# A trunk of RWKV-7 and dilated attention: gate weights loaded into a freed mix, one panel beside the weight ring, the bias copies in six parts

## The chip, the cores and the metric

The kernel runs on one core of one Trainium2 chip. The core has five engines that run side by side, each through its own list of instructions: TensorE (PE in the profile; matmuls, with PEld for the loads of its stationary operand), VectorE (DVE), ScalarE (ACT), GpSimd (POOL) and SyncE (SP), which here only issues DMAs. They wait for each other by semaphores. The metric is the device time of one launch in microseconds; a kernel's time is the median of several runs.

## What is computed

One RWKV-7 time-mixing layer, a feed-forward layer, one dilated-attention layer and a second feed-forward layer, on 512 tokens of width 1024. The change lies in the first of them and in the data that the attention's bias needs:

```python
xx = jnp.pad(h, ((0, 0), (1, 0), (0, 0)))[:, :-1] - h
x_mix = h[None] + xx[None] * mu[:, None, None, :]
r, k, v = (x_mix[c] @ w_rkv[c] for c in range(3))
xw, xa, xg = x_mix[3], x_mix[4], x_mix[5]
w = -jax.nn.softplus(-(w0 + jnp.tanh(xw @ w1) @ w2)) - 0.5
decay = jnp.exp(-jnp.exp(w))
a = jax.nn.sigmoid(a0 + (xa @ a1) @ a2)
g = jax.nn.sigmoid(xg @ g1) @ g2
...
y = rwkv7_scan(r, decay, k, v, -kk, kk * a)     # state, token by token
out = ((group_norm(y) + bonus) * g) @ w_o
...
logits = logits + bias[None, None, None]        # attention: a bias by head and distance
```

Here `w1`, `a1`, `g1` are the first, narrow halves of the decay, removal and output gates (64, 64 and 160 columns), `w2`, `a2`, `g2` the second ones.

## The kernel before

**First projections.** The activations lie transposed, in eight chunks of 128 rows by 512 tokens. The weights come as *panels* of 128 x 1024 numbers (512 KB, `stream[p]`), each the weights of one output tile: panels 0 to 2 for the first keys and values, 3 to 10 for the receptance, 11 (`PAN_WA`) for the decay and removal gates together, 12 and 13 (`PAN_G`) for the output gate. From 14 on (`PAN_PROJ`) come the keys and values of the later head pairs. SP loads panel p into slot p mod 2 of a ring, `O_RAW`, as soon as the panel that had the slot, p - 2, is through. For most panels that means "split": ScalarE rounds the panel to a high half (`split_high`) and VectorE subtracts that to get the low half (`split_low`), both into rings of three, and TensorE takes 24 matmuls for a tile (`product`). A few panels, 11 and those from 14 on among them, are read by TensorE straight from the ring, and there the slot is free when the tile is done (semaphore `dense`). Tiles go alternately into two PSUM banks, which ScalarE empties (`take`); the next tile but one waits for that (`freed`).

Panel 11's tile is `decay_and_gate` on TensorE; ScalarE empties it in two pieces, Tanh for the decay half and a plain copy for the other. Tiles 12 and 13 are emptied with Sigmoid. ScalarE holds one set of function tables at a time, and a change of set is an instruction of its own (ACT_TABLE_LOAD).

**The loop.** Then a loop over k from -1 to 8 works on the eight head pairs, with parts of three pairs interleaved: `gates`, `key_norm_ready`, `first_inverse`, the scores and so on of pair k+1, the inverse of pair k, the walk over the chunks of pair k-1. I call the loop body with k = 0 round 0. Into it are spread `project(k, 0)` to `project(k, 15)`, eight matmul steps each of two further panels, which keep TensorE busy between the small matmuls. The order on each engine is written out by hand; nothing is scheduled afterwards.

The gates' second weights (`lora_out`) come in pieces of 128 KB per head pair, two slots for the decay and removal gates (`O_LWA`, `gate_weights`) and two for the output gate (`O_LWG`, `output_gate_weights`). SP issues them, and the constants of the loop (`O_CM`, "the mask", with the reset pattern that VectorE's scan and GpSimd's start wait for), after the last projection tile.

**The bias.** The attention layer far behind needs every bias row of 384 numbers 128 times, shifted; for that 48 rows in DRAM (`bias_rows`) are copied 128 times each into `bias_copies`, by three DMAs from DRAM to DRAM of 3072 KB. They too stand in SP's list, behind the first gate weights; SP waits for them when the attention layer starts.

Of the kernel before, what the change touches and what calls it, by code (L numbers as in the profile page):

```python
# [160 lines left out]
O_LWA = O_CM + N_CM  # L161
O_LWG = O_LWA + 2 * 2 * P
O_AR = O_LWG + 2 * 2 * P
# [7 lines left out]
O_EP = O_CC + S  # L171
# [54 lines left out]
def trunk(nc, xT, stream, lora_out, pvec, const, rel33, out):  # L226
    with ExitStack() as ctx:
# [178 lines left out]

        def full(eng, t):

            eng.wait_ge(s["dense"], TILE_AT[t])
# [7 lines left out]
        def _(sp):  # L417
# [7 lines left out]
            def panel(p):  # L425
                if p >= RAW and is_split(p - RAW):
                    sp.wait_ge(s["w_lo"], split_of(p - RAW) + 1)
                elif p >= RAW:
                    sp.wait_ge(s["dense"], PANEL_AT[p - RAW])
                sp.dma_start(f(O_RAW + p % RAW * 1024, 1024), stream[p]).then_inc(s[f"w_raw{p % RAW}"], 16)  # L430

            for p in range(PAN_PROJ + RAW):
                panel(p)
                if p == 1:
                    sp.dma_start(f(O_OH, 3 * 384, 0, 33), const[0:33, C_OH:C_OH + 3 * 384]).then_inc(s["oh_in"], 16)
                    sp.dma_start(f(O_REL, 48, 0, 33), rel33).then_inc(s["oh_in"], 16)
                    sp.dma_start(con(C_ID), const[:, C_ID:C_ID + P]).then_inc(s["con_in"], 16)
                    sp.dma_start(con(C_HEAD, 2 * P), const[:, C_HEAD:C_HEAD + 2 * P]).then_inc(s["con_in"], 16)
            full(sp, T_WO0 - 1)
            sp.dma_start(f(O_CM, N_CM), const[:, C_SCORE:C_OH]).then_inc(s["mask_in"], 16)  # L440

# [12 lines left out]
            gate_weights(0)  # L454
            gate_weights(1)
            output_gate_weights(0)
            output_gate_weights(1)
            sp.wait_ge(s["bias_dma"], 48)
            for g in range(3):
                rows = bias_rows[g * 16 * 384:(g + 1) * 16 * 384]  # L460
                copies = bias_copies[g * 16 * P * 384:(g + 1) * 16 * P * 384]
                sp.dma_start(copies.rearrange("(h i u) -> h i u", h=16, i=P),
                             bass.AP(tensor=rows.tensor, offset=g * 16 * 384, ap=[[384, 16], [0, P], [1, 384]]))\
                    .then_inc(s["bias_rep"], 16)
            for k in range(-1, NHP - 1):
# [1662 lines left out]
```

## Time and profile before

| | |
|---|---|
| median of 3 runs | 1932.83 us (1930.52 to 1936.12) |
| the profiled execution | 1931.57 us, of it 1929.8 us span |
| granted TensorE clock, mean | 0.972 of 2.4 GHz |
| TensorE busy | 1821.2 us (94%), 15682 matmul records |
| VectorE, ScalarE, GpSimd busy | 932.1, 781.3, 203.8 us |
| DMA | 155.04 MB, mean 80 GB/s |
| `bias_copies` from `bias_rows` | 3 DMAs of 3072.0 KB |

A matmul in fp32 shows as two records, each of about the length of one pass. In the timelines equal instructions that follow each other are merged, with their number behind an x; what stands in brackets is the idle time of the engine just before, and what ended it. A line L503 or L506 is a helper through which every matmul goes, so groups of matmuls are known by their time, number and shape. For SP the length of a row runs from the first of its issues to the end of the last, waits between them included. The granted clock is 1.00 at 2.4 GHz and 0.50 at 1.2 GHz.

### The profile page before, as it was taken

The numbers are of one execution on the slowest core, as the hardware profiler recorded it, in microseconds if no ns is written. First come the engines' busy times: TensorE is split into PE (matmuls) and PEld (weight loads), VectorE is DVE, ScalarE is ACT, GpSimd is POOL, SyncE is SP. The second block draws the span as 40 slices with busy tenths as digits, with TensorE's granted clock in tenths as the row PEclk, the third lists the DMA queues.
The fourth block names the chain that finished last, engine by engine and source line by source line (L and its number), as shares of the span: only waits on it lengthen the run. The fifth ranks groups of instructions, "written<-read, shape, count | busy, mean of one in ns | idle before, by whom it ended". The sixth has DMA issues, their size and how long they took to land.

```text
span 1929.8 us, 36430 instructions
## 1 busy us (share of the span) xinstructions
PE 1821.2 (94%) x15682; PEld 1407.4 (73%) x15682; DVE 932.1 (48%) x1585; ACT 781.3 (40%) x1326; POOL 203.8 (11%) x180
## 2 busy tenths in 40 slices
PE   8978999987799999999999999999999799999999
PEld 3745555655578888888887777777787688888887
DVE  6624555555444444434445554654654554444422
ACT  4333444434233222322446556556656543222211
POOL 0022333334110000000010111111111000000000
PEclk9989999987789999999999999999999899999999
DMA  3281111000222233323232222222222133323322
GB/s 121 77 260 43 34 30 30 28 16 3 70 72 94 97 98 98 99 99 98 88 99 77 77 68 76 77 77 66 79 75 77 33 99 98 99 88 102 100 95 97
DMA packets 57544, 155.04 MB, mean 80 GB/s; under 512 B 5591, under 2 KB 22535, under 8 KB 57384
## 3 DMA queue, kind: packets, MB, share of 16 engines
q1 hardware_dynamic: 57288, 152.63, 24.6%
q8 instruction: 125, 2.05, 0.4%
q14 instruction: 35, 0.29, 0.0%
q10 hardware_dynamic: 96, 0.07, 0.0%
HBM read 150.51 MB, written 11.61 MB: 84 GB/s over the span
## 4 chain that ended last, share of the span: by engine, by line
PE 67%; ACT 4%; issue 1%; DVE 0%; POOL 0%; ACTq 0%; DVEq 0%
PE bank L503 66%; PE bank L506 2%; ACT f L1433 2%; ACT f L1446 1%; ACT f L1420 0%; ACT r L1411 0%; ACT f L1407 0%; ACT f L1438 0%; POOL f L2045 0%; POOL f L2049 0%; DVE f L1899 0%; POOL f L2047 0%; DVE f L1910 0%; DVE r L1916 0%; DVE f L1697 0%
## 5 line engine op out<-in xcount | busy, mean ns | idle before, releaser
L503 PE MATMUL bank<-r 128*128 128x512 f32 x5616 | 1304.2, 392 | 7.0 <-DVE r L1916 3.7
L503 PEld LDWEIGHTS bank<-r 128*128 128x128 f32 x5616 | 1050.9, 188 | 241.3 <-issue 18.1
L503 PE MATMUL bank<-f 64*64 64x64 f32 (+6 forms) x9634 | 475.5, 259 | 78.2 <-DVE f L1637 16.6
L503 PEld LDWEIGHTS bank<-f 64*64 64x64 f32 (+3 forms) x9634 | 308.1, 146 | 235.3 <-issue 110.7
L1506 DVE TENSOR_TENSOR r<-f,r 128x1024 fp32r<-128x1024 f32 x230 | 282.9, 1231 | 390.4 <-ACT r L1122 390.4
L1122 ACT ACTIVATE r<-f 128x1024 fp32r<-128x1024 f32 x230 | 240.7, 1047 | 151.6 <-PE bank L503 138.2
L2074 POOL TENSOR_TENSOR r<-f,r 128x512 fp32r<-128x512 f32 x48 | 62.2, 1295 | 885.8 <-ACT r L1411 885.8
L1390 ACT ACTIVATE r<-f 128x512 fp32r<-128x512 f32 x44 | 27.8, 632 | 218.1 <-DVE f L1809 218.1
L1840 DVE TENSOR_TENSOR f<-bank,f 128x512 f32<-128x512 f32 x72 | 56.0, 777 | 87.6 <-PE bank L503 84.7
L1637 DVE TENSOR_TENSOR f<-bank,f 64x512 f32<-64x512 f32 x80 | 55.1, 689 | 66.6 <-PE bank L503 65.4
L506 PE MATMUL bank<-f 128*128 128x128 f32 x432 | 65.4, 281 | 20.2 <-ACT f L1446 14.3
L506 PEld LDWEIGHTS bank<-f 128*128 128x128 f32 x432 | 49.0, 141 | 42.2 <-ACT f L1446 26.7
L1420 ACT ACTIVATE f<-bank,f 128x512 f32<-128x512 f32 x48 | 32.9, 686 | 100.0 <-PE bank L503 100.0
L1387 ACT ACTIVATE f<-f 128x512 f32<-128x512 f32 x44 | 27.8, 632 | 112.4 <-DVE f L1799 112.4
L1446 ACT ACTIVATE f<-bank 128x512 f32<-128x512 f32 (+1 forms) x64 | 36.4, 568 | 89.6 <-PE bank L506 89.6
L1803 DVE TENSOR_TENSOR f<-bank,f 128x512 f32<-128x512 f32 x44 | 30.4, 691 | 78.8 <-PE bank L503 78.8
L1433 ACT ACTIVATE f<-f 128x256 f32<-128x256 f32 (+1 forms) x128 | 61.4, 481 | 2.3 <-DVE f L1882 2.3
L1856 DVE SCALAR_TENSOR_TENSOR f<-f 128x512 f32<-128x512 f32 x32 | 37.3, 1166 | 39.5 <-ACT f L1422 39.5
L1873 DVE CUSTOM_DVE_ANT_0 f<-bank,f 128x256 f32<-128x256 f32 (+1 forms) x128 | 44.4, 404 | 11.8 <-PE bank L503 11.7
L1194 ACT ACTIVATE f<-bank 128x512 f32<-128x512 f32 (+1 forms) x48 | 27.7, 594 | 53.6 <-PE bank L503 38.3
L1376 ACT ACTIVATE r<-f 128x512 fp32r<-128x512 f32 x24 | 15.2, 633 | 83.0 <-DVE f L1782 83.0
L1645 DVE COPY f<-bank 128x512 f32<-128x512 f32 (+1 forms) x40 | 27.5, 689 | 42.7 <-PE bank L503 42.7
(108 smaller groups left out, 959.5 us busy)
## 6 DMA issues: line engine op xcount, KB each, us to landing
f<-stream SPq DMA_DIRECT2D x247, 512.0 KB, 3.4
bias_copies<-bias_rows SPq DMA_DIRECT2D x3, 3072.0 KB, 24.7
f<-xT SPq DMA_DIRECT2D x16, 256.0 KB, 4.3
f<-lora_out SPq DMA_DIRECT2D x16, 128.0 KB, 3.7
f<-bias_copies SPq DMA_DIRECT2D x16, 128.0 KB, 3.2
f<-bias_copies SPq DMA_DIRECT2D x32, 64.0 KB, 2.9
outT<-f SPq DMA_DIRECT2D x8, 256.0 KB, 4.5
f<-const SPq DMA_DIRECT2D x1, 576.0 KB, 3.7
```

Of the source, the lines that this page charges most:

```text
L503: return nc.tensor.matmul(out, lhsT, rhs, start=start, stop=stop, skip_group_check=True)
L506: return nc.tensor.transpose(out, in_, con(C_ID))
L1122: A(r(O_WHI + q % PAN * 1024, 1024), f(O_RAW + p % RAW * 1024, 1024), ACT.Copy)\
L1420: free(A(f(O_QS), banks[4][:, :], ACT.Ln, bias=kol(K_EPS), scale=1.0 / HD), 4)
L1433: A(tile, tile, ACT.Exp, bias=f(sm + 8 + n, 1), accum_out=f(sm + 16 + n, 1))\
L1446: free(A(f(O_PT + n % N_PT * S, w), banks[5][:, 0:w], ACT.Copy), 5)
L1506: TT(r(O_WLO + q % PAN * 1024, 1024), f(O_RAW + panel_of(q) % RAW * 1024, 1024), rf(O_WHI + q % PAN * 1024, 1024), ALU.subtract).then_inc( ...
L1637: TT(bc(half(O_XI, e), (CH, 8), (1, CH)), banks[2 + e][CH * e:CH * (e + 1), :].rearrange("p (t j) -> p t j", t=8), bc(lev, (0, 8), (1, CH) ...
L1840: TT(out, in0, in1, ALU.mult).then_inc(freed(t), 1)
L1856: STT(by_residue(to), bc(f(O_QR + n % 2 * S), (4, P), (1, 4)), gain, bc(f(O_QS), (4, P), (1, 4)), ALU.mult, ALU.mult).then_inc(s["qk_norm" ...
L1873: ins = V.tensor_tensor_reduce(out=f(O_P + h * 4 * S + n * 2 * P + first, w), in0=banks[b][:, e * 2 * P + first:(e + 1) * 2 * P], in1=f(O_ ...
L2074: TT(r(O_QL), f(O_QQ), rf(O_QH), ALU.subtract).then_inc(s["q_sq_lo"], 1)
```

## The change

Panel 11 is loaded into `O_TG`, the place in which the output gate's Sigmoid results are put later, with a semaphore of its own (`w_wa`). It no longer takes a slot of the ring, so panel 13 waits for panel 9, the last one that had its slot; the ring's counts are one lower from there on for that slot (`raw_in`). The slots for `lora_out` move into the place of the receptance mix (`O_XM`), which is free when tile 10 is done, and their first four loads are issued there, before panel 14. ScalarE loads the sigmoid tables before it waits for tile 11, copies first, then takes Tanh, and splits panel 13 behind that. The three copies become six of half the size, issued one in each of rounds 0 to 5 behind the round's panels.

```diff
@@ places in SBUF
-O_LWA = O_CM + N_CM
-O_LWG = O_LWA + 2 * 2 * P
-O_AR = O_LWG + 2 * 2 * P
+O_AR = O_CM + N_CM
...
-O_EP = O_CC + S
+O_LWA = O_CC + S
+O_LWG = O_LWA + 2 * 2 * P
+O_EP = O_LWG + 2 * 2 * P
+assert O_XM <= O_LWA and O_EP <= O_XM + KC * S
@@ all engines
+        def raw_in(eng, p):
+            early = p > PAN_WA and (p - PAN_WA) % RAW == 0
+            eng.wait_ge(s[f"w_raw{p % RAW}"], 16 * (p // RAW + 1 - early))
@@ SP
             def panel(p):
-                if p >= RAW and is_split(p - RAW):
-                    sp.wait_ge(s["w_lo"], split_of(p - RAW) + 1)
-                elif p >= RAW:
-                    sp.wait_ge(s["dense"], PANEL_AT[p - RAW])
+                held = p - RAW - (RAW if p - RAW == PAN_WA else 0)
+                if p == PAN_WA:
+                    sp.dma_start(f(O_TG, 1024), stream[p]).then_inc(s["w_wa"], 16)
+                    return
+                if held >= 0 and is_split(held):
+                    sp.wait_ge(s["w_lo"], split_of(held) + 1)
+                elif held >= 0:
+                    sp.wait_ge(s["dense"], PANEL_AT[held])
...
             for p in range(PAN_PROJ + RAW):
+                if p == PAN_PROJ:
+                    full(sp, PAN_WA - 1)
+                    for hp in range(2):
+                        gate_weights(hp)
+                        output_gate_weights(hp)
                 panel(p)
...
-            gate_weights(0)
-            gate_weights(1)
-            output_gate_weights(0)
-            output_gate_weights(1)
-            sp.wait_ge(s["bias_dma"], 48)
-            for g in range(3):
-                rows = bias_rows[g * 16 * 384:(g + 1) * 16 * 384]
-                copies = bias_copies[g * 16 * P * 384:(g + 1) * 16 * P * 384]
-                sp.dma_start(copies.rearrange("(h i u) -> h i u", h=16, i=P),
-                             bass.AP(tensor=rows.tensor, offset=g * 16 * 384, ap=[[384, 16], [0, P], [1, 384]]))\
+            def copy_bias(n):
+                lo = n * 8 * 384
+                copies = bias_copies[lo * P:(lo + 8 * 384) * P]
+                sp.dma_start(copies.rearrange("(h i u) -> h i u", h=8, i=P),
+                             bass.AP(tensor=bias_rows.tensor, offset=lo, ap=[[384, 8], [0, P], [1, 384]]))\
                     .then_inc(s["bias_rep"], 16)
             for k in range(-1, NHP - 1):
                 if k + 3 < NHP:
                     gate_weights(k + 3)
                 for p in (PAN_PROJ + 2 * (k + 2), PAN_PROJ + 2 * (k + 2) + 1):
                     if p < PAN_WO0 + RAW:
                         panel(p)
+                if 0 <= k < 6:
+                    if k == 0:
+                        sp.wait_ge(s["bias_dma"], 48)
+                    copy_bias(k)
                 if k >= 1:
                     output_gate_weights(k + 1)
@@ TensorE, decay_and_gate
-                pe.wait_ge(s[f"w_raw{t % RAW}"], 16 * (t // RAW + 1))
+                pe.wait_ge(s["w_wa"], 16)
...
-                    w = O_RAW + t % RAW * 1024 + c * P
+                    w = O_TG + c * P
@@ ScalarE
-                split_high(min(t + LEAD, PAN_PROJ - 1))
+                if t != PAN_WA:
+                    split_high(min(t + LEAD, PAN_PROJ - 1))
                 for i in MIXED_AT.get(t, []):
                     round_mixed(i)
                 if t == PAN_WA:
+                    nc.scalar.preload_act_table_set("sigmoid_and_others")
                     full(act, t)
-                    A(f(O_TW, S, 0, LORA), banks[t % 2][0:LORA, :], ACT.Tanh)
-                    A(f(O_TA, S, LORA, P), banks[t % 2][LORA:P, :], ACT.Copy).then_inc(freed(t), 1)
+                    A(f(O_TA, S, LORA, P), banks[t % 2][LORA:P, :], ACT.Copy)
+                    A(f(O_TW, S, 0, LORA), banks[t % 2][0:LORA, :], ACT.Tanh).then_inc(freed(t), 1)
+                    split_high(PAN_PROJ - 1)
```

The rest of the diff puts `raw_in` in the places where TensorE and ScalarE waited for a ring slot, and doubles the count that SP waits for before the attention's bias (`bias_rep`, 96 for 48).

SP's list before, from panels 5 to 12 in the first row, panel 13 in the second, to the loads of the first pass of the loop (a stream row is a panel; the 128x1152 row is the mask; of `lora_out`, L445 is `gate_weights` and L451 `output_gate_weights`):

```order
L430 DMA f<-stream 128x1024 [waits w_lo] x8
L430 DMA f<-stream 128x1024 [waits dense]
L430 DMA f<-stream 128x1024 [waits w_lo] x2
L440 DMA f<-const 128x1152 [waits dense]
L445 DMA f<-lora_out 128x2x128 x2
L451 DMA f<-lora_out 128x2x128 x2
L462 DMA bias_copies<-bias_rows 2048x1x384 [waits bias_dma]
L462 DMA bias_copies<-bias_rows 2048x1x384 x2
L445 DMA f<-lora_out 128x2x128 [waits a_ps]
L430 DMA f<-stream 128x1024 [waits dense] x2
```

The same stretch of SP's list now; L434 is panel 11, and the row behind it is panels 12 and 13:

```order
L440 DMA f<-stream 128x1024 [waits w_lo] x6
L434 DMA f<-stream 128x1024
L440 DMA f<-stream 128x1024 [waits w_lo] x2
L445 DMA f<-lora_out 128x2x128 [waits dense]
L451 DMA f<-lora_out 128x2x128
L445 DMA f<-lora_out 128x2x128
L451 DMA f<-lora_out 128x2x128
L440 DMA f<-stream 128x1024 [waits w_lo] x2
L467 DMA f<-const 128x1152 [waits dense]
L445 DMA f<-lora_out 128x2x128 [waits a_ps]
L440 DMA f<-stream 128x1024 [waits dense] x2
```

The four gate weights stand before panels 14 and 15 and the mask, where they stood behind them, and panel 13 waits for a low half (`w_lo`) where it waited for tile 11 (`dense`). The copies are gone from here.

SP's list now, from the loads of round 0 through those of round 2:

```order
L445 DMA f<-lora_out 128x2x128 [waits a_ps]
L440 DMA f<-stream 128x1024 [waits dense] x2
L474 DMA bias_copies<-bias_rows 1024x1x384 [waits bias_dma]
L445 DMA f<-lora_out 128x2x128 [waits a_ps]
L440 DMA f<-stream 128x1024 [waits dense] x2
L474 DMA bias_copies<-bias_rows 1024x1x384
L451 DMA f<-lora_out 128x2x128 [waits g_ps]
```

Each copy stands behind the two panels of its round, and before the output gate's weights where there are any.

ScalarE's list before, from tile 9 to the first gates (L1158 is `take`, L1122 the split of panels 12 and 13, L1140 the rounding of the output gate's mix, L1186 and L1187 Tanh and the copy, L1194 the gates' Sigmoid):

```order
L1158 ACTIVATE f<-bank 128x512 [waits dense]
L1122 ACTIVATE r<-f 128x1024 [waits dense,w_raw0]
L1140 ACTIVATE r<-f 128x512 [waits mix_t] x2
L1158 ACTIVATE f<-bank 128x512 [waits dense]
L1122 ACTIVATE r<-f 128x1024 [waits dense,w_raw1]
L1186 ACT_TABLE_LOAD
L1186 ACTIVATE f<-bank 64x512 [waits dense]
L1187 ACTIVATE f<-bank 64x512
L1158 ACT_TABLE_LOAD
L1158 ACTIVATE f<-bank 128x512 [waits dense] x2
L1204 ACTIVATE f<-f 128x512 [waits tile_free1,tile_free0]
L1194 ACTIVATE f<-bank,f 128x512 [waits w_ps]
```

The same stretch now (L1175, L1139, L1157, L1205 the copy, L1206 Tanh, L1214):

```order
L1175 ACTIVATE f<-bank 128x512 [waits dense]
L1139 ACTIVATE r<-f 128x1024 [waits dense,w_raw0]
L1157 ACTIVATE r<-f 128x512 [waits mix_t] x2
L1175 ACTIVATE f<-bank 128x512 [waits dense]
L1203 ACT_TABLE_LOAD
L1205 ACTIVATE f<-bank 64x512 [waits dense]
L1206 ACTIVATE f<-bank 64x512
L1139 ACTIVATE r<-f 128x1024 [waits dense,w_raw1]
L1175 ACTIVATE f<-bank 128x512 [waits dense] x2
L1224 ACTIVATE f<-f 128x512 [waits tile_free1,tile_free0]
L1214 ACTIVATE f<-bank,f 128x512 [waits w_ps]
```

The split of panel 13 has moved behind Tanh and the copy, these two have changed places, the first table load stands ahead of the wait for `dense`, and the second is gone.

## Rows read from the trace of the kernel before

**Rows 1.** Part 4 of the page, the chain by engine.

```profile
PE 67%; ACT 4%; issue 1%; DVE 0%; POOL 0%; ACTq 0%; DVEq 0%
```

**Rows 2.** Timeline of TensorE, 95 to 300: start, us, instructions, [idle before <- releaser].

```profile
95.98 5.85 PE L503 MATMUL bank<-r 128*128 128x512 f32 x24
103.41 5.85 PE L503 MATMUL bank<-r 128*128 128x512 f32 x24 [1.57 <-ACT f L1187]
113.56 2.08 PE L503 MATMUL bank<-f 64*128 64x512 f32 x4 [4.31 <-DMA f<-lora_out]
116.38 11.37 PE L503 MATMUL bank<-f 128*128 128x512 f32 x20 [0.74 <-ACT f L1194]
128.53 7.97 PE L503 MATMUL bank<-f 128*128 128x512 f32 x140 [0.78 <-ACT f L1316]
...
143.12 1.16 PE L503 MATMUL bank<-f 64*64 64x64 f32 x64 [2.13 <-ACT f L1194]
149.29 7.71 PE L503 MATMUL bank<-f 128*128 128x512 f32 x110 [5.00 <-DMA f<-stream]
...
193.57 7.92 PE L503 MATMUL bank<-f 64*64 64x64 f32 x198 [2.13 <-ACT f L1194]
...
240.27 9.52 PE L503 MATMUL bank<-f 64*64 64x64 f32 x198 [2.13 <-ACT f L1194]
```

**Rows 3.** Windows: length, busy time of engines, granted clock, DMA share, GB/s.

```profile
116.38:121.58 5.20, 5.20 (x6) 2.16 (x7) 2.77 (x3) 3.26 (x5) 3.09 (x3) 0.51 1.04 325
121.58:143.12 21.54, 18.22 (x195) 8.42 (x193) 5.64 (x9) 4.49 (x9) 10.08 (x9) 1.00 0.98 316
149.29:153.00 3.71, 3.71 (x32) 2.56 (x36) 0.00 (x0) 0.25 (x1) 0.00 (x0) 0.61 0.02 8
143.12:187.37 44.25, 37.39 (x953) 24.91 (x953) 20.81 (x32) 15.85 (x30) 12.28 (x11) 0.92 0.14 45
193.57:231.94 38.37, 36.99 (x1037) 25.23 (x1037) 23.43 (x41) 17.58 (x33) 15.11 (x14) 1.00 0.07 19
```

**Rows 4.** Timeline of ScalarE, 95 to 130.

```profile
99.79 1.06 ACT L1122 ACTIVATE r<-f 128x1024 fp32r<-128x1024 f32 x1 [10.12 <-DMA f<-stream]
100.87 1.28 ACT L1186 ACT_TABLE_LOAD   x1
102.16 0.59 ACT L1186 ACTIVATE f<-bank 64x512 f32<-64x512 f32 x1
...
109.30 0.60 ACT L1158 ACTIVATE f<-bank 128x512 f32<-128x512 f32 x1 [4.03 <-PE bank L503]
```

**Rows 5.** Timeline of SP's DMA issues, 40 to 700.

```profile
109.29 0.33 SPq L440 DMA_DIRECT2D f<-const  x1
...
111.68 14.52 SPq L462 DMA_DIRECT2D bias_copies<-bias_rows  x3
126.24 11.28 SPq L445 DMA_DIRECT2D f<-lora_out  x1
137.56 2.75 SPq L430 DMA_DIRECT2D f<-stream  x2
...
170.06 20.68 SPq L430 DMA_DIRECT2D f<-stream  x2
...
214.93 22.50 SPq L430 DMA_DIRECT2D f<-stream  x2
```

**Rows 6.** Timeline of VectorE, 105 to 200.

```profile
113.10 0.17 DVE L1701 TENSOR_SCALAR f<-f 128x8 f32<-128x8 f32 x1 [10.99 <-DMA f<-const]
...
119.10 1.22 DVE L1590 TENSOR_TENSOR_SCAN f<-f 128x512 f32<-128x512 f32 x1
```

**Rows 7.** Timeline of GpSimd, 105 to 200.

```profile
117.11 0.77 POOL L1983 TENSOR_SCALAR f<-f 128x512 f32<-128x512 f32 x1 [116.67 <-ACT f L1194]
...
120.39 1.06 POOL L1993 TENSOR_TENSOR f<-f 128x512 f32<-128x512 f32 x1 [1.17 <-DVE f L1590]
...
126.21 1.27 POOL L2013 TENSOR_TENSOR f<-f 128x512 f32<-128x512 f32 x1
```

More of the change, by code:

```diff
@@ L425, in panel @@
             def panel(p):
-                if p >= RAW and is_split(p - RAW):
-                    sp.wait_ge(s["w_lo"], split_of(p - RAW) + 1)
-                elif p >= RAW:
-                    sp.wait_ge(s["dense"], PANEL_AT[p - RAW])
-                sp.dma_start(f(O_RAW + p % RAW * 1024, 1024), stream[p]).then_inc(s[f"w_raw{p % RAW}"], 16)
[L432 to L440, printed above, removed]
+                held = p - RAW - (RAW if p - RAW == PAN_WA else 0)
[6 more added lines that the diff above has]
+                    sp.wait_ge(s["dense"], PANEL_AT[held])
+                sp.dma_start(f(O_RAW + p % RAW * 1024, 1024), stream[p]).then_inc(s[f"w_raw{p % RAW}"], 16)
             def gate_weights(hp):
@@ L452, in output_gate_weights @@
                              lora_out[:, 2:4, hp * P:(hp + 1) * P]).then_inc(s[f"lwg_in{hp % 2}"], 16)
-            gate_weights(0)
-            gate_weights(1)
-            output_gate_weights(0)
-            output_gate_weights(1)
-            sp.wait_ge(s["bias_dma"], 48)
-            for g in range(3):
-                rows = bias_rows[g * 16 * 384:(g + 1) * 16 * 384]
-                copies = bias_copies[g * 16 * P * 384:(g + 1) * 16 * P * 384]
-                sp.dma_start(copies.rearrange("(h i u) -> h i u", h=16, i=P),
-                             bass.AP(tensor=rows.tensor, offset=g * 16 * 384, ap=[[384, 16], [0, P], [1, 384]]))\
+            for p in range(PAN_PROJ + RAW):
+                if p == PAN_PROJ:
[3 more added lines that the diff above has]
+                        output_gate_weights(hp)
+                panel(p)
+                if p == 1:
+                    sp.dma_start(f(O_OH, 3 * 384, 0, 33), const[0:33, C_OH:C_OH + 3 * 384]).then_inc(s["oh_in"], 16)
+                    sp.dma_start(f(O_REL, 48, 0, 33), rel33).then_inc(s["oh_in"], 16)
+                    sp.dma_start(con(C_ID), const[:, C_ID:C_ID + P]).then_inc(s["con_in"], 16)
+                    sp.dma_start(con(C_HEAD, 2 * P), const[:, C_HEAD:C_HEAD + 2 * P]).then_inc(s["con_in"], 16)
+            full(sp, T_WO0 - 1)
+            sp.dma_start(f(O_CM, N_CM), const[:, C_SCORE:C_OH]).then_inc(s["mask_in"], 16)
+            def copy_bias(n):
[3 more added lines that the diff above has]
+                             bass.AP(tensor=bias_rows.tensor, offset=lo, ap=[[384, 8], [0, P], [1, 384]]))\
                     .then_inc(s["bias_rep"], 16)
@@ L482, in _ @@
                     if hp == 0 and h == 0:
-                        sp.wait_ge(s["bias_rep"], 48)
+                        sp.wait_ge(s["bias_rep"], 96)
                         sp.wait_ge(s["hd_lo"], FC)
@@ L547, in plain @@
                     pe.wait_ge(freed(t), t // 2)
-                pe.wait_ge(s[f"w_raw{t % RAW}"], 16 * (t // RAW + 1))
+                raw_in(pe, t)
                 for c in range(KC):
@@ L556, in decay_and_gate @@
                 pe.wait_ge(freed(t), t // 2)
-                pe.wait_ge(s[f"w_raw{t % RAW}"], 16 * (t // RAW + 1))
+                pe.wait_ge(s["w_wa"], 16)
                 for c in range(KC):
@@ L587, in project @@
                 if c == 0:
-                    pe.wait_ge(s[f"w_raw{p % RAW}"], 16 * (p // RAW + 1))
+                    raw_in(pe, p)
                     if n:
@@ L1118, in split_high @@
                     p = panel_of(q)
-                    act.wait_ge(s[f"w_raw{p % RAW}"], 16 * (p // RAW + 1))
+                    raw_in(act, p)
                     if q >= PAN:
```

## The prediction

> **What bounds the kernel now.** I read the page first: the chain that ended last runs for 67% of the span through TensorE's matmuls, and no other engine has more than 4% of it [rows 1]. So only a stretch in which TensorE waits, or in which its clock is low, can give time back. The change touches the end of the first projections and the first round of the RWKV loop, so the second view is TensorE's timeline there [rows 2]. The reader is to see three waits. Tile 13, the last projection tile (24 matmuls), starts 1.57 us after tile 12 ended and waits for ScalarE's line 1187. The first four matmuls of the loop, from the decay and gate weights, start 4.31 us after tile 13 and wait for a load of lora_out. And in round 0 TensorE is done with 64 small matmuls at 144.28 and then waits 5.00 us for a panel of stream.
>
> The third view is a set of windows [rows 3]: the granted clock is at 0.51, the 1.2 GHz level, from 116.38 to 121.58 behind the first two waits, at 1.00 from there to 143.12, and at 0.61 on average from 149.29 to 153.00 behind the third wait. Round 0 from its 64 matmuls to its scores takes 44.25 us; round 1, with more matmuls in it, 38.37.
>
> The fourth view is who holds TensorE up. On ScalarE [rows 4] the split of panel 13 stood in front of Tanh. It began at 99.79 after 10.12 us of waiting for the panel, whose load could only start when the decay tile, tile 11, was through with the slot; a table load of 1.28 us followed, and only then Tanh and the copy that free the bank. On SP [rows 5] the mask is asked for when tile 13 ends (109.29) and the gate weights behind it. Then three copies occupy SP for 14.52 us and the next gate weights for 11.28 more, so the panel that round 0 needs at 144.28 is asked for at 137.56 and is there at 149.29. Each of these causes is something that the change moves.
>
> **Tile 13 without its wait.** Panel 11 goes outside the ring, so panel 13 waits only for panel 9 and is in place long before. The sigmoid table is loaded ahead of the wait for tile 11, where ScalarE waits anyway; copy, Tanh and split follow. From tile 11's end, about 96.0 (the next row starts at 95.98), I count two evacuations of 0.59 (the row at 102.16), the split of 1.06, and for VectorE's half as much as for ScalarE's: 3.3 us, so the weights are ready at 99.3 and tile 12 ends at 95.98 + 5.85 = 101.83. Tile 13 starts there: 1.57 us saved, with 2.5 us of cover left. The second table load, between Tanh and Sigmoid, is gone; it lay beside tile 13 and counts nothing.
>
> **The loop's start without the load.** The four loads of lora_out are asked for when tile 10 ends; two whole tiles and tile 13 lie between that and their use. What remains late is ScalarE's evacuation of tile 13: 0.04 + 0.60 [rows 4], and about 0.13 for the signal. Tile 13 ends at 101.83 + 5.85 = 107.68, so the four matmuls start at 108.45 instead of 113.56, 5.11 us earlier with the 1.57 in it. The loads now stand on SP ahead of panels 14 and 15, which start later by four issues; the mask's issue took 0.33, and these panels are needed after 111. No cost.
>
> **The clock.** With 0 and 0.77 us of waiting in place of 1.57 and 4.31, I take it that TensorE keeps 2.4 GHz. The rows bound it: the four matmuls cost 2.08 at the low level and half, 1.04, at the high one; the 5.20 us at 0.51 become 2.60. Behind the four, TensorE still waits 0.74 for ScalarE. So the block of 20 passes starts at 108.45 + 1.04 + 0.74 = 110.23, takes 11.37 - 2.60 = 8.77 and ends at 119.00; with the 0.78 behind it the next block starts at 119.78 and not at 128.53.
>
> **What is late next there.** The mask is still asked for at the end of tile 13, 109.26 before. VectorE had it 3.84 us later [rows 6], so now at 107.68 + 3.84 = 111.52, and GpSimd can start 0.17 + 0.23 later, at 111.92, though ScalarE would let it start at 111. Its chain to the scaled vectors that the first inverse needs (the product that ends at 126.21 + 1.27 = 127.48) took 10.37 us from 117.11 [rows 7], of which 1.17 were a wait for VectorE's scan. The scan ended at 120.32, 3.94 after the block of 20 began; now at 114.2 at the latest, when GpSimd asks for it at about 114.0. That leaves 9.2 us: 121.15. TensorE would get there at 119.78 plus two passes (0.88), 120.66, and waits half a microsecond. Before, it got there at 129.41 and found the product ready. **Gain up to here: 129.41 - 121.15 = 8.26 us.**
>
> **Round 0 without the panel's wait.** The panel is asked for when its slot is free, at 119.0, with no copy in front. Even if it took the 11.7 us of before it would be there at 130.7, and it is needed at about 136.0 (144.28 less 8.26). The 5.00 us go, and with them the low clock behind: (1 - 0.61) x 3.71 = 1.45. **6.45 us.** Rounds 0 and 1 compared give 44.25 - 38.37 = 5.88 with more work in round 1, which fits.
>
> **The copies, one a round.** The trace has no copy of the new size. Three old ones took SP 14.52, 4.84 each; a new one takes between half of that and all of it, and I take half. SP has room: the second panel of a pair is out by 190.74 and the next panel is asked for at 214.93 [rows 5]. The bytes, 1.57 MB at the 325 GB/s of the first window in [rows 3], take 4.8 us. The panel in front of a copy is needed when the next round is half through its projection, which is also when the next panel is asked for, 24 us later. So I cost the copies at nothing; a gain is excluded, as rounds from 1 on have no such wait to lose, and the far end is rival C.
>
> **The sum.** 8.26 + 6.45 = 14.71. The profiled execution took 1931.57 us (span 1929.8), 1.26 below the median of 1932.83 and within the runs shown: 1931.57 - 14.71 = 1916.86, so 1917. What lies behind round 0 is a chain that starts from it and moves along.
>
> **Rivals.**
> B, the clock stays low. Four waits of 0.5 to 0.8 us remain between 107 and 121, and one of 2.13 in every round [rows 2]. Behind such a wait the same 198 matmuls take 7.92 us in round 1 and 9.52 in round 2, 1.60 more. If the first stretch stays at 1.2 GHz, its gain is 5.11 and not 8.26, and if round 0 falls as round 2 did, 1.60 more goes: 5.11 + 6.45 - 1.60 = 9.96, 1921.6. For it: TensorE is at the low level here now. Against it: the wait of 0.78 at 128.53 left the clock at 1.00. The Trainium skill (TensorE: Matmul & The Clock Gate, "A second HAM failure mode: psum-queue depth-cycling") says that TensorE can swing between its two clocks when it idles briefly between groups of matmuls; by that rule B's 1921.6 stands in place of 1917. The trace agrees for the 2.13 us waits in some rounds and not for the shorter ones, which is why B has the smaller chance.
>
> C, the copies get in the way of panels: slower. They share the queue. If each of the six did to a round what the three did to round 0, that would cost 6 x 6.45 = 38.7: 1916.9 + 38.7 = 1955.6. It decides from the point where a panel beside a copy lands more than 24 us after its request; in round 0 one took 11.7 behind what was left of three copies of twice the size, which speaks against it. The Trainium skill (DMA: Bandwidth & Descriptors, "Queues, rings and completion order") says that a DMA engine takes what one issuer queued in ring order; the trace agrees in so far as that panel came late behind the copies. By that rule C's 1955.6 stands wherever the cover is shorter than I read.
>
> D, another wait takes a removed one's place: the panel's turns into one for ScalarE's copy of the projected key, or GpSimd's chain is longer than 9.2. Half the gain is left, 6.5 to 8.3 us: 1923 to 1925. Against it: in round 1 the same 64 matmuls are followed by others without a wait.
>
> E, later low-clock stretches swallow it, as they need not fall on the same rounds when all is earlier: 1.6 us each, three or four of them against the change. With D's half gain that is no change, about 1930.
>
> **Chances.** The forecast 0.67, its own range 1911 to 1922 (three such stretches either way, and the scatter of the runs); B 0.16; D 0.09; E 0.04; C 0.04. About 0.3%, 5.8 us, is what this measurement can tell from no change. Faster: 0.67 + 0.16 + 0.07 of D = 0.90; same 0.06; slower 0.04. The range is 1910 to 1924, with B inside.
>
> **What would show it.** Right: tile 13 follows tile 12 without a wait; under 1 us in front of the loop's first four matmuls; the full clock from 108 to 121; the block that began at 128.53 begins near 119.8; no wait for stream in round 0, and some 38 us for it; one table load, ahead of Tanh. Wrong: a clock near 0.5 from 110 to 118 (B), a wait for stream in rounds 1 to 6 (C), one of several us for ScalarE or GpSimd in round 0 (D), or later rounds that grew (E).

## The result and the profile after

The changed kernel takes 1918.91 us (median of 4 runs, 1914.41 to 1919.21), the kernel before 1933.38 (4 runs, 1930.52 to 1936.12). The ratio is 0.992, 95% interval 0.9899 to 0.9941: 14.5 us are gone. The profiled execution took 1919.21 us, of it 1917.4 span; against the profiled one of before, 1931.57, that is 12.4 less. A second set of runs is among the experiments (a1): 0.9922 (0.9909 to 0.9935).

The chain of the page says what it said before [rows 1], with one point more for TensorE:

```profile
PE 68%; ACT 4%; issue 1%; DVE 0%; POOL 0%; ACTq 0%; DVEq 0%
```

TensorE's timeline from tile 12 on answers to [rows 2]:

```profile
96.65 11.42 PE L520 MATMUL bank<-r 128*128 128x512 f32 x48
108.80 1.13 PE L520 MATMUL bank<-f 64*128 64x512 f32 x4 [0.73 <-issue]
110.67 6.28 PE L520 MATMUL bank<-f 128*128 128x512 f32 x14 [0.74 <-ACT f L1214]
117.43 2.81 PE L520 MATMUL bank<-f 128*128 128x512 f32 x6 [0.48 <-DVE f L1626]
...
122.78 6.94 PE L520 MATMUL bank<-f 64*64 64x64 f32 x138 [0.66 <-POOL f L2033]
130.14 4.08 PE L520 MATMUL bank<-f 64*64 64x128 f32 x40 [0.42 <-issue]
136.34 8.97 PE L520 MATMUL bank<-f 64*64 64x64 f32 x174 [2.13 <-ACT f L1214]
...
181.96 7.92 PE L520 MATMUL bank<-f 64*64 64x64 f32 x198 [2.13 <-ACT f L1214]
...
275.94 9.50 PE L520 MATMUL bank<-f 64*64 64x64 f32 x198 [2.13 <-ACT f L1214]
```

Tiles 12 and 13 are one row now, 48 matmuls without a wait. The loop's first four matmuls follow 0.73 us behind, and no row waits for a load of lora_out or for a panel of stream. The first inverse, which began at 129.41 (two matmuls into the row of 128.53), begins at 122.78, and the scores (the row of 40) at 130.14, where before they began at 136.91. All of this stands 0.67 us late from tile 12 on (96.65 for 95.98), which I don't count to the change: tile 11, in front of it, began anywhere from 88.30 to 90.28 in profiled executions below whose instructions up to there are the same as here (89.63). I take the 0.67 out where I compare places; the whole time has it in it.

The windows (columns as in [rows 3]):

```profile
97.00:122.78 25.78, 22.39 (x75) 12.94 (x73) 7.29 (x7) 10.28 (x17) 9.22 (x8) 1.00 0.21 67
136.34:175.75 39.41, 37.64 (x953) 25.32 (x953) 20.81 (x32) 15.86 (x30) 12.29 (x11) 0.96 0.06 17
181.40:190.30 8.90, 8.35 (x204) 6.26 (x205) 5.80 (x10) 5.28 (x8) 3.09 (x3) 1.00 0.56 200
```

The granted clock is 1.00 in the whole first stretch, where it was 0.51 for 5.20 us. Round 0 takes 39.41 us and not 44.25, but at a clock of 0.96. The last row is the stretch of the first copy, whose packets run from 181.39 to 190.29; I come back to it.

ScalarE beside tiles 11 to 13, for [rows 4]:

```profile
90.35 1.28 ACT L1203 ACT_TABLE_LOAD   x1
96.77 0.59 ACT L1205 ACTIVATE f<-bank 64x512 f32<-64x512 f32 x1 [5.13 <-PE bank L520]
97.37 0.59 ACT L1206 ACTIVATE f<-bank 64x512 f32<-64x512 f32 x1
97.86 1.05 ACT L1139 ACTIVATE r<-f 128x1024 fp32r<-128x1024 f32 x1
```

The table load stands inside ScalarE's wait for tile 11, and copy, Tanh and split follow each other from 96.77. VectorE's half of that split is this row:

```profile
98.94 1.22 DVE L1526 TENSOR_TENSOR r<-f,r 128x1024 fp32r<-128x1024 f32 x1 [9.12 <-ACT r L1139]
```

SP's issues, for [rows 5]:

```profile
91.18 0.47 SPq L451 DMA_DIRECT2D f<-lora_out  x1
91.69 8.84 SPq L440 DMA_DIRECT2D f<-stream  x2
108.10 0.33 SPq L467 DMA_DIRECT2D f<-const  x1
...
120.27 13.24 SPq L440 DMA_DIRECT2D f<-stream  x2
...
179.17 0.75 SPq L474 DMA_DIRECT2D bias_copies<-bias_rows  x1
```

The panels of round 0 are asked for from 120.27 to 133.51, with nothing in front, and the copies go out behind the panels of later rounds, at 179.17 first, where one takes SP 0.75 us. VectorE in the first stretch, for [rows 6]:

```profile
111.91 0.17 DVE L1721 TENSOR_SCALAR f<-f 128x8 f32<-128x8 f32 x1 [11.74 <-DMA f<-const]
...
112.59 1.63 DVE L1610 TENSOR_TENSOR_SCAN f<-f 128x512 f32<-128x512 f32 x1
114.14 1.68 DVE L1621 SCALAR_TENSOR_TENSOR f<-f 128x512 f32<-128x512 f32 x1
115.74 1.54 DVE L1626 SCALAR_TENSOR_TENSOR f<-f 128x512 f32<-128x512 f32 x1
```

GpSimd in the same stretch, for [rows 7]:

```profile
112.38 0.77 POOL L2003 TENSOR_SCALAR f<-f 128x512 f32<-128x512 f32 x1 [111.94 <-DVE f L1721]
113.23 2.04 POOL L2007 TENSOR_TENSOR f<-f 128x512 f32<-128x512 f32 x1
115.24 1.50 POOL L2013 TENSOR_TENSOR f<-f 128x512 f32<-128x512 f32 x1
...
121.37 1.26 POOL L2033 TENSOR_TENSOR f<-f 128x512 f32<-128x512 f32 x1
```

Here is the part that did not go by plan. The scan took 1.22 us before [rows 6] and takes 1.63. GpSimd's product beside it (L2007) takes 2.04, and its next one (L2013) 1.50, which took 1.06 [rows 7]. VectorE's unit key (L1621) takes 1.68. In the kernel before, that first product and the unit key were these:

```profile
117.96 1.26 POOL L1987 TENSOR_TENSOR f<-f 128x512 f32<-128x512 f32 x1
120.64 1.36 DVE L1601 SCALAR_TENSOR_TENSOR f<-f 128x512 f32<-128x512 f32 x1 [0.32 <-ACT f L1218]
```

### The profile page after: what moved, and what is told of

Read it like the earlier page. It is cut to its first block, busy times and chain, and to the rows that moved or that the text cites. A ratio compares the mean times of both kernels' runs of the same rounds, so it can differ in the third digit from the quotient of the medians.

```text
span 1917.4 us, 36432 instructions
## 1 busy us (share of the span) xinstructions
PE 1816.0 (95%) x15682; PEld 1404.8 (73%) x15682; DVE 933.5 (49%) x1585; ACT 779.8 (41%) x1325; POOL 204.9 (11%) x180
## 4 chain that ended last, share of the span: by engine, by line
PE 68%; ACT 4%; issue 1%; DVE 0%; POOL 0%; ACTq 0%; DVEq 0%
PE bank L520 66%; PE bank L523 2%; ACT f L1453 2%; ACT f L1466 1%; ACT f L1440 0%; ACT r L1431 0%; ACT f L1427 0%; ACT f L1458 0%; POOL f L2065 0%; POOL f L2069 0%; DVE f L1919 0%; POOL f L2067 0%; DVE r L1936 0%; DVE f L1930 0%; DVE f L1717 0%
## 5 line engine op out<-in xcount | busy, mean ns | idle before, releaser
L520 PE MATMUL bank<-f 64*64 64x64 f32 (+6 forms) x9634 | 470.6, 258 | 72.6 <-DVE f L1657 16.9
L1139 ACT ACTIVATE r<-f 128x1024 fp32r<-128x1024 f32 x230 | 240.7, 1047 | 143.0 <-PE bank L520 138.1
L1860 DVE TENSOR_TENSOR f<-bank,f 128x512 f32<-128x512 f32 x72 | 56.0, 778 | 87.6 <-PE bank L520 84.7
L1823 DVE TENSOR_TENSOR f<-bank,f 128x512 f32<-128x512 f32 x44 | 30.4, 692 | 78.8 <-PE bank L520 78.8
L1819 DVE TENSOR_TENSOR f<-bank,f 128x512 f32<-128x512 f32 x44 | 30.4, 692 | 35.0 <-PE bank L520 29.1
L1214 ACT ACTIVATE f<-bank 128x512 f32<-128x512 f32 (+1 forms) x48 | 27.7, 594 | 47.0 <-PE bank L520 32.1
```

The source lines that it names most:

```text
L520: return nc.tensor.matmul(out, lhsT, rhs, start=start, stop=stop, skip_group_check=True)
L1139: A(r(O_WHI + q % PAN * 1024, 1024), f(O_RAW + p % RAW * 1024, 1024), ACT.Copy)\
L1860: TT(out, in0, in1, ALU.mult).then_inc(freed(t), 1)
```

## The experiments

Each kernel was timed in rounds with the kernel before on the same chip; ratios are to that, with the 95% interval. The times named in the expectations are for a chip on which the kernel before takes 1933 us, so gains are compared, not times. The kernels of a group shared a chip: e1 to e4 (before: 1930.03 us); a1, e5, e6 and e8 (1932.21); e7, e9 and e10 (1928.64). The [rows] named here are those ahead of the prediction.

**e1, the copies in front again.** The changed kernel, with the three old copies at their old place.

```diff
+            sp.wait_ge(s["bias_dma"], 48)
+            for g in range(3):
+                rows = bias_rows[g * 16 * 384:(g + 1) * 16 * 384]
...
-                if 0 <= k < 6:
-                    if k == 0:
-                        sp.wait_ge(s["bias_dma"], 48)
-                    copy_bias(k)
```

> The kernel after, but with the three old copies at their old place, behind the mask and ahead of the loop's loads. Theory (the parts depend on each other): the copies start some 3 us earlier than before, so the panel of round 0 lands near 146 while TensorE wants it near 137; the 8 us won ahead of it turn into a longer wait for stream, about 8.6 us. Gain against before only 3 to 4 us, about 1930. Rival (the parts simply add): 8.3 us won stay, 6.45 of round 0 are not: about 1925.

Measured: 1926.3 us, 0.9985 (0.9971 to 0.9999). TensorE in its round 0:

```profile
135.44 1.16 PE L515 MATMUL bank<-f 64*64 64x64 f32 x64 [2.13 <-ACT f L1209]
144.31 7.95 PE L515 MATMUL bank<-f 128*128 128x512 f32 x110 [7.72 <-DMA f<-stream]
```

SP's issues before that, in the same kernel:

```profile
107.45 13.24 SPq L474 DMA_DIRECT2D bias_copies<-bias_rows  x3
120.74 11.46 SPq L445 DMA_DIRECT2D f<-lora_out  x1
```

By the times 3 to 4 us are gained, as the theory has it and not the rival's 8.3. The whole first stretch is early, as in the changed kernel: the scores of the first pass start at 129.23, 7.68 before those of the kernel before. Part of that is lost in round 0: the panel lands at 144.3, TensorE is there at 136.6 and waits 7.72, and the scores of round 0 are 4.68 early (182.69 for 187.37). The panel of before landed at 149.29 [rows 2]. So the early start alone is worth little, because the panel's time is set by the copies.

**e2, the copies alone.** The kernel before, with the copies one a round.

```diff
-            for g in range(3):
-                rows = bias_rows[g * 16 * 384:(g + 1) * 16 * 384]
...
+            def copy_bias(n):
+                lo = n * 8 * 384
...
+                if 0 <= k < 6:
+                    if k == 0:
+                        sp.wait_ge(s["bias_dma"], 48)
+                    copy_bias(k)
```

> The kernel before with nothing but the copies moved: six of half the size, one a round. Theory: the 5.00 us wait for stream in round 0 and 1.45 us of low clock behind it go, nothing else: 6.45 us, about 1927. The first two waits (1.57 and 4.31) and the low clock behind them stay. Rival (the copies moved into the rounds cost something there, a wait for stream or lora_out in rounds 1 to 6): less than 5 us gained, 1929 or more. Together with the run without moved copies, the theory says that the two gains add up to some 10 us, not to the 14.5 of both.

Measured: 1923.62 us, 0.9968 (0.9955 to 0.998), 6.2 to 6.4 us less. TensorE's timeline:

```profile
103.36 5.85 PE L508 MATMUL bank<-r 128*128 128x512 f32 x24 [1.53 <-ACT f L1192]
113.50 1.81 PE L508 MATMUL bank<-f 64*128 64x512 f32 x4 [4.29 <-DMA f<-lora_out]
...
142.52 7.43 PE L508 MATMUL bank<-f 64*64 64x64 f32 x174 [2.13 <-ACT f L1199]
```

The two waits of the first stretch stand, the one for stream is gone, and round 0 from 142.52 to its scores at 180.71 takes 38.19 us. The term of 6.45 is confirmed by itself. With e1, the two parts alone give 3 and 6 us, 9 or 10 together, and both at once 14.5 to 15: much of the first part's gain is paid out only when the second has removed the wait behind it.

**e3, the gate weights late.** The changed kernel, with the four lora_out loads behind the mask again.

```diff
-                if p == PAN_PROJ:
-                    full(sp, PAN_WA - 1)
-                    for hp in range(2):
-                        gate_weights(hp)
-                        output_gate_weights(hp)
...
+            gate_weights(0)
+            gate_weights(1)
+            output_gate_weights(0)
+            output_gate_weights(1)
```

> The kernel after, but the four first loads of lora_out at their old place, behind the mask. Theory: TensorE waits some 4.3 us for lora_out before the loop, and its clock falls behind that: the four matmuls take 2 us and the block behind them stays half-way at the low level, so the loss is 3.5 for the wait and up to 3 for the clock, 6 us, about 1925. Rival: the first inverse is bound by the mask and GpSimd's chain, not by TensorE, so most of it is hidden: TensorE's clock falls but the loss is 2 to 4 us, about 1922.

Measured: 1921.51 us, 0.9959 (0.9946 to 0.9971). TensorE:

```profile
112.09 2.08 PE L519 MATMUL bank<-f 64*128 64x512 f32 x4 [4.34 <-DMA f<-lora_out]
114.92 10.79 PE L519 MATMUL bank<-f 128*128 128x512 f32 x20 [0.74 <-ACT f L1213]
```

The wait for lora_out is back, and with it the low clock: the granted clock is 0.50 from 112.09 to 116.00, the four matmuls take 2.08 for 1.13, the block behind them 10.79. The scores come at 134.86, 4.7 us later than in the changed kernel, 5.0 with tile 11 set to the same place. By the ratios (0.9959 for 0.9922 in a1) it is 7 us, which is the theory's 6 rather than the rival's 2 to 4; the 2 us by which this is more than in the trace are not accounted for. This is the largest piece of the first stretch, and its loss of clock goes with it.

**e4, panel 11 in the ring.** The changed kernel, with panel 11 in the ring and ScalarE's old order at tile 11.

```diff
-            early = p > PAN_WA and (p - PAN_WA) % RAW == 0
+            early = 0
...
-                    nc.scalar.preload_act_table_set("sigmoid_and_others")
...
-                    A(f(O_TA, S, LORA, P), banks[t % 2][LORA:P, :], ACT.Copy)
-                    A(f(O_TW, S, 0, LORA), banks[t % 2][0:LORA, :], ACT.Tanh).then_inc(freed(t), 1)
-                    split_high(PAN_PROJ - 1)
+                    A(f(O_TW, S, 0, LORA), banks[t % 2][0:LORA, :], ACT.Tanh)
+                    A(f(O_TA, S, LORA, P), banks[t % 2][LORA:P, :], ACT.Copy).then_inc(freed(t), 1)
```

> The kernel after, but panel 11 in the ring and ScalarE's old order around Tanh with its two table loads. Theory: the wait of 1.57 us in front of tile 13 is back, and nothing else changes: about 1920.5, clock at 1.00 until 121. Rival: with 1.57, 0.75 and 0.75 us of waiting close together the clock falls to 0.5 there and the loss is 3 to 5 us: 1922 to 1924.

Measured: 1918.23 us, 0.9943 (0.9928 to 0.9959). TensorE:

```profile
104.01 5.86 PE L516 MATMUL bank<-r 128*128 128x512 f32 x24 [1.54 <-ACT f L1200]
```

Tile 13 waits 1.54 us, the scores come at 131.90, 1.76 later, and the clock stays at 1.00 from 104 to 124.55. By the trace the step is worth what it was given, 1.6; by the time (0.9943 against 0.9922 for a1 below, with intervals that overlap) that can't be told from nothing. The ring and ScalarE's order are undone together here, so which of the two brings the wait back is not shown.

**a1, the changed kernel again**, for the kernels of the second group.

> The kernel after, unchanged, as the measure for the runs beside it and for the four that went before, on a chip whose kernel before takes about 1930. Theory: ratio 0.992 to 0.993 as at first, about 1916; the panel in the ring cost 1.6 us of that, the late gate loads 5 to 6, the copies in front 10. In its trace VectorE's scan takes near 1.6 us and GpSimd's product beside it near 2.0, as at first (1.22 and 1.26 in the kernel before).

Measured: 1915.86 us (1915.44 to 1918.59), 0.9922 (0.9909 to 0.9935).

**e5, the reset pattern early.** The pattern that the scan and GpSimd's start wait for is cut off the mask and loaded with the gate weights, so that GpSimd starts when ScalarE lets it.

```diff
+                    sp.dma_start(f(O_RESET), const[:, C_RESET:C_OH]).then_inc(s["reset_in"], 16)
...
-            dve.wait_ge(s["mask_in"], 16)
+            dve.wait_ge(s["reset_in"], 16)
...
-            pool.wait_ge(s["mask_in"], 16)
```

> The kernel after, with the mask cut in two: the reset pattern that the scan reads (512 columns) goes into a further part of the freed receptance mix and is loaded with the gate weights; the other 640 columns come when the mask came, and VectorE and GpSimd wait for them only at the first inverse. Theory (the mask holds up GpSimd's start): GpSimd starts some 1 us earlier, at 111.4 on the first trace's times instead of 112.38, and TensorE's first inverse is 1.0 to 1.3 us earlier: about 1 us faster than the kernel after. Rival (VectorE and GpSimd slow each other when they run at the same time, and that sets the chain): the start is earlier but the scan and the product beside it take as long or longer, and less than 0.5 us comes of it.

Measured: 1916.62 us, 0.992 (0.9903 to 0.9938), no difference to a1. VectorE's scan in it:

```profile
111.77 2.17 DVE L1613 TENSOR_TENSOR_SCAN f<-f 128x512 f32<-128x512 f32 x1
```

GpSimd's first three operations in it:

```profile
110.74 0.77 POOL L2007 TENSOR_SCALAR f<-f 128x512 f32<-128x512 f32 x1 [110.30 <-ACT f L1217]
111.59 1.27 POOL L2011 TENSOR_TENSOR f<-f 128x512 f32<-128x512 f32 x1
114.02 1.48 POOL L2017 TENSOR_TENSOR f<-f 128x512 f32<-128x512 f32 x1 [1.16 <-DVE f L1613]
```

GpSimd starts 0.96 us earlier (tile 11 set to the same place), and its product takes 1.27, but the scan beside it takes 2.17, GpSimd's next product waits 1.16 for that, and the first inverse gains only 0.55. The mask is not the whole of the lateness.

**e8, GpSimd's product behind the scan.** One wait more in the first pass, so that the product and the scan don't overlap.

```diff
+                if hp == 0:
+                    pool.wait_ge(s["cs"], 1)
```

> The kernel after, but for the first head pair GpSimd waits for VectorE's scan before its second operation, the product that ran beside the scan. Theory (two engines slow each other): the scan goes back to 1.2 us from 1.6 and GpSimd's product to about 1.3 from 2.0, so that the chain ends no later, within 0.7 us. Rival (they do not; the long times are due to something else at this place): both keep their long times and the chain ends about 1 us later.

Measured: 1915.45 us, 0.9918 (0.9905 to 0.9932). The scan still took 1.64, as GpSimd's operation ahead of the product (L2003, 0.77) lay beside its first half; the product took 1.64, now beside the unit key (L1621), which took 0.73. GpSimd's chain took 10.54 against 10.25. It overlaps elsewhere, and decides nothing; hence the next one.

**e10, GpSimd behind VectorE's key.** GpSimd starts when VectorE's scan and unit key (L1621) are both done.

```diff
+                else:
+                    pool.wait_ge(s["kk"], 1)
```

> The kernel after, but for the first head pair GpSimd starts only when VectorE is through with the maximum, the scan and the unit key. Theory (VectorE and GpSimd slow each other where they overlap): VectorE's scan takes 1.2 and the unit key 0.75 now that nothing runs beside them, GpSimd's first product 1.3 instead of 2.0; the start is some 2 us later and the first inverse 1 to 2 us later. Rival (the place makes them long, not the overlap): scan 1.6, product 2.0 as in the kernel after, the first inverse 2 to 3 us later.

Measured: 1918.38 us, 0.995 (0.9934 to 0.9966). VectorE in it:

```profile
112.53 1.22 DVE L1610 TENSOR_TENSOR_SCAN f<-f 128x512 f32<-128x512 f32 x1
114.06 0.75 DVE L1621 SCALAR_TENSOR_TENSOR f<-f 128x512 f32<-128x512 f32 x1 [0.32 <-ACT f L1238]
```

GpSimd in it, its product and the next one:

```profile
115.89 1.26 POOL L2009 TENSOR_TENSOR f<-f 128x512 f32<-128x512 f32 x1
117.11 1.06 POOL L2015 TENSOR_TENSOR f<-f 128x512 f32<-128x512 f32 x1
```

The scan is back at 1.22, the two products at 1.26 and 1.06 as before, and the unit key takes 0.75 (1.68 in the changed kernel; 1.36 before, where it also lay beside a GpSimd operation). So what lengthened them is that they ran beside each other. It is no gain, since the wait costs more: the first inverse comes 1.4 us later than in a1 (124.22 for 122.90, tile 11 at 89.51 and 89.61). The ratio is some 5 us above a1's, with intervals that barely overlap; what the trace does not account for of that stays open.

**e6, every copy twice.** Each copy is issued a second time, into a spare tensor.

```diff
-                    copy_bias(k)
+                    copy_bias(k, bias_copies)
+                    copy_bias(k, bias_spare)
```

> The kernel after, with every one of the six copies issued twice, the second time into a spare tensor that nothing reads. Theory (the copies lie wholly beside the rounds): no difference from the kernel after, no wait for stream or lora_out on TensorE in rounds 1 to 6. Rival (they get in the way of panels as soon as there are more bytes): a wait for stream in the second half of rounds 1 to 6, some us each, 10 us or more in all.

Measured: 1922.66 us (1914.4 to 1925.05), 0.9944 (0.9926 to 0.9963), about 4 us more than a1 with intervals that overlap. TensorE's waits from 80 to 430 (total us, times, longest), in the changed kernel:

```profile
PE bank L520 <- ACT f L1214: 15.6, 8, 2.1
...
PE bank L520 <- issue: 5.6, 11, 1.0
```

And in this one:

```profile
PE bank L523 <- issue: 10.4, 18, 1.3
```

In neither whole list is there a wait for stream, so even doubled the copies hold up no panel. What grew is time in which TensorE waited for nothing that the profile shows, by 4.8 us. Neither the theory nor the rival had that in it. a1 has 6.8 there, and the other profiled executions have 3.3 to 7.3, so some 3 to 5 us go with the second copies; the longest that the changed kernel doesn't have end at 240.91, 245.43, 291.82 and 339.21, and the two copies of a round end at 242.7, 291.2 and 340.0. That TensorE's own instructions come late while copies run is my reading, and argued only. The profiled execution took 1916.06, no more than a1, as one round alone fell to the low clock in it.

**e7, three copies of full size in rounds 0 to 2.**

```diff
-                lo = n * 8 * 384
+                lo = n * 16 * 384
...
-                if 0 <= k < 6:
+                if 0 <= k < 3:
```

> The kernel after, but the copies keep their old size: three, one in each of rounds 0 to 2. Theory (it matters only that they are out of the way when round 0 asks for its panel): same as the kernel after within 2 us; each copy moves its 3 MB in 10 to 12 us with all DMA engines at work where the halves move 1.5 MB in 8.5 with half of them. Rival (the size matters: 3 MB in one round are too much, as with the copies issued twice): 3 to 6 us slower, with more waits of TensorE for its own instructions in rounds 1 to 3.

Measured: 1918.22 us (1910.94 to 1922.39), 0.9942 (0.9923 to 0.9962). The runs scatter by 11 us, and the time doesn't tell whether six parts are better than three. TensorE waited 7.3 us for nothing visible from 80 to 430, near a1's 6.8. The window of the first copy of 16 rows, whose packets run from 182.54 to 192.68:

```profile
182.50:192.70 10.20, 9.50 (x198) 6.88 (x199) 5.17 (x9) 5.14 (x8) 3.10 (x3) 0.83 0.96 327
```

It moves twice the bytes in 10.1 us, at a DMA share of 0.96 and 327 GB/s, where the changed kernel's copy of 8 rows took 8.9 us at 0.56 and 200 (181.4 to 190.3, above).

**e9, the tables each round.** Not an undoing but the change's own trick carried on: it loads ScalarE's tables ahead of a wait once; here it is done in every round, ahead of the wait for the gates.

```diff
             def gates(hp):
                 if hp:
+                    nc.scalar.preload_act_table_set("sigmoid_and_others")
                     act.wait_ge(s["cs"], hp)
```

> The kernel after, with its own step for Tanh done in every round as well: ScalarE loads the sigmoid tables of the gates ahead of the wait for TensorE's gate matmuls, not behind it. Theory: the 2.13 us that TensorE waits for ScalarE in each of seven rounds are a table load (1.28) and a Sigmoid with its signals (0.85), so 1.28 us go in each, 9.0 in all, and with waits of 0.85 the clock falls less often in rounds 0 to 5 (1.6 us each time, about three times a run): 9 to 13 us under the kernel after, 1903 to 1907. Rival (something else is late next: the unit matrices from GpSimd, or the copy of the projected key): less than 5 us.

Measured: 1903.58 us (1902.27 to 1904.81), 0.9869 (0.9855 to 0.9884), below both kernels. TensorE in two of its rounds:

```profile
135.10 7.43 PE L520 MATMUL bank<-f 64*64 64x64 f32 x174 [0.85 <-ACT f L1214]
...
177.39 7.92 PE L520 MATMUL bank<-f 64*64 64x64 f32 x198 [0.85 <-ACT f L1214]
```

ScalarE in it, from the first pass to the gates of round 0:

```profile
121.53 1.28 ACT L1228 ACT_TABLE_LOAD   x1
134.36 1.27 ACT L1214 ACTIVATE f<-bank,f 128x512 f32<-128x512 f32 x2 [11.54 <-PE bank L520]
```

The load of 1.28 us, which in the changed kernel followed the wait and stood in front of the gates (134.31 to 135.59), lies in ScalarE's idle time, and TensorE's wait falls from 2.13 to 0.85 in each round, by just that. From the scores row of the first pass to that of round 4 the changed kernel took 234.09 us (130.14 to 364.23), this one 222.54 (130.17 to 352.71): 11.55 less, of which five loads are 6.4, and three rounds that fell to the low clock there and not here 4.55 (1.54, 1.58 and 1.43 by their 174 and 198 matmuls). In this execution no round up to round 5 falls to the low clock. That the shorter wait is what kept the clock up is not shown: by the ratios e9 is 10 us under a1, of which seven loads of 1.28 are 9.0, and the mean granted clock of its four runs is 0.980 to 0.981, against 0.979 to 0.981 in a1's four.

## Why the prediction was right, point by point

The forecast was 1917.0 from a gain of 14.71; the medians give 14.5, and a1's ratio 15.1. The time itself, 1918.91, is 1.9 above the forecast, which was taken off the profiled execution's 1931.57 and not off the median. The profiled pair gives 12.4, and that one can be taken apart.

**Tile 13: right.** No wait; the weights are ready at 98.94 + 1.22 = 100.16 by VectorE's row for the split, 3.5 us after tile 11's end (3.3 expected), against 101.83 + 0.67 when tile 13 starts. e4 puts the wait back and finds 1.54.

**The loop's start and its clock: right.** The four matmuls start at 108.80, 0.3 us earlier than 108.45 + 0.67, and take 1.13. The clock was the riskiest term, and e3 shows that it hangs on the lora_out wait and not on tile 13's: with 4.34 us of waiting the low level is back, with 1.54 (e4) it isn't. Rival B's first half did not come about.

**GpSimd's chain: the mis-sized term.** I gave it 9.2 us from GpSimd's start; it took 10.25 (112.38 to 122.63). The first inverse began at 122.78 - 0.67 = 122.11 and not at 121.15, so 0.96 too late, and up to the scores the gain is 136.91 - 130.14 + 0.67 = 7.44, not 8.26. My start was right (111.92 against 112.38 - 0.67 = 111.71). What I missed is that VectorE also waits for the mask, so both engines start together and lie beside each other for the next 5 us, while in the kernel before GpSimd waited out the scan. I took GpSimd's durations from rows in which its operations ran nearly alone. e10 shows it: apart, each takes what it took. VectorE's operations also grew: TensorE got a new wait of 0.48 for L1626 from it.

**Round 0: the panel's wait right, the clock wrong in this execution.** The 5.00 us are gone, and e2 measures the term alone with 6.2 to 6.4 of 6.45. In the profiled execution round 0 took 39.41 us and not 37.80, since the 174 matmuls behind the wait of 2.13 took 8.97 us and not 7.43: 1.54 for the low clock. That is the second half of rival B, and which rounds fall varies by execution: before, rounds 2, 3 and 5 fell, after it rounds 0, 3 and 4, in a1, the same kernel, rounds 0, 2 and 4, in e6 round 4 alone of the first six. Round 0 fell in five of the nine profiled executions of the changed kernel and of its variants that keep the wait of 2.13 and have no wait for the panel (in this one, a1, e5, e7 and e10; not in e3, e4, e6 and e8). So my sum took the better of two cases; the worse one stood only in rival B and in the range.

**The copies: hidden, but by less than I reckoned.** I let 1.57 MB flow at 325 GB/s in 4.8 us; the first copy's packets take 8.9, at 200 GB/s with what runs beside them. The 24 us of cover are still well over twice that. Rival C is out: no wait for stream in any round, not even doubled (e6).

**The sum.** With tile 11 at the same place the two terms measure 7.44 and 4.84, against 8.26 and 6.45; the chain's lateness and the low clock of round 0 are what is missing. The profiled 12.4 has the 0.67 in it besides: as they stand, the scores of the first pass come 6.77 earlier and those of round 0 11.62 (175.75 for 187.37), and 0.8 more comes behind that. There the kernel before fell to the low clock in three of rounds 1 to 5 and the changed one in two, which is 1.6, while round 1 became 0.6 longer. So 14.71 less 0.82, 1.61 and 0.67, plus 0.8, is the 12.4. That the gain of the medians agrees with the forecast's within 0.2 us is partly luck: my sum took the better case for round 0 and too short a chain, and the interval of the ratio allows a gain of 11 to 20 us. Rival D was there in kind, a longer GpSimd chain, but took 1 us and not the 6 to 8 that it was given; of E nothing is seen, as three of the first six rounds fell in either profiled execution.

## What to carry to other kernels

An early start is worth only what the next transfer lets through: here 3 and 6 us alone made 14.5 to 15 together, so price two such edits as a pair, from the stretch behind. When a removed wait lets two engines start at once that took turns before, don't take their durations from the rows in which each ran alone. And look for table loads that stand behind a semaphore wait: moved ahead of it, one a round, they were worth 10 us here, about two thirds of what the whole change gave (e9).

## What the runs showed of the hardware

**VectorE and GpSimd take turns.** In the overlaps of this stretch the one that came second ended about when the other's end plus its own duration would have it. In e5 the product ran undisturbed from 111.59 to 112.86; a scan of 1.22 behind that would end at 114.08, and it ended at 113.94. In the changed kernel GpSimd's first operation ended at 113.15, the scan at 114.22 (114.37 if it took its turn then), the product behind that at 115.27 (115.48), the key at 115.82 (116.02), GpSimd's second product at 116.74 (116.88). So each is 0.1 to 0.2 us earlier than strict turns. The Trainium skill (SBUF — State Buffer, "SBUF: two separate sides") says that VectorE and GpSimd share a pair of ports as an exclusive lock, which whoever starts first has for the whole instruction, and that a VectorE operation with two inputs in SBUF takes part in this when the GpSimd operation reads SBUF. The trace agrees, up to that 0.1 to 0.2 us.

**Eight rows, half the engines.** The copy of 8 rows took 8.9 us, the one of 16 rows 10.1, with DMA shares of 0.56 and 0.96 in their windows, loads that lie beside them included. In the trace 7.7 packets of the first are under way on average, and 14.5 of the second. The Trainium skill (DMA: Bandwidth & Descriptors, "Why a DMA increments its semaphore by 16 and not by 1") says that a DMA is spread over the largest number of engines up to 16 that divides the outermost dimension of both sides, here 8 and 16. The packets under way agree with that. Halving a copy in this way saved little of its time.

**The clock after a wait of 2.13 us is not settled by the wait.** The same wait was followed by 7.92 us for 198 matmuls in one round and by 9.50 in another of the same execution, and which rounds it hits changes from run to run of one kernel (rounds 0, 3 and 4 in the changed kernel, 0, 2 and 4 in a1). With 0.85 us it hit none of rounds 0 to 5 in the one profiled execution of e9.
